# A two-model transformer forward on one core: the last MLP's second product with tokens on the output partitions

## The reference

```python
h = h + jnp.square(jax.nn.relu(rmsnorm(h, g) @ w_up)) @ w_down   # w_up [1024, 4096], w_down [4096, 1024]
return h * rsqrt(mean(h * h, axis=-1) + 1e-6) * final_norm_g
```

## Time and profile before

| | us |
|---|---|
| median of 3 runs | 1107.19 (1106.84 to 1107.58) |
| profiled execution | 1107.31 |
| its span | 1105.6 |
| TensorE busy | 1095.7 (99%) |
| VectorE busy | 780.3 (71%) |
| ScalarE busy | 608.8 (55%) |
| w1's first product, last product's start | 1006.55, 1095.59 |

### The profile page before, as it was taken

The page is one execution under the profiler, slowest core; times in us unless marked ns, Lnnn a source line. Parts: engine busy times, 40 slices in busy tenths (PEclk is TensorE's granted clock), DMA queues, the critical chain, the costliest instruction groups (busy, mean ns, idle before and its releaser), DMA issues.

```text
span 1105.6 us, 19232 instructions
## 1 busy us (share of the span) xinstructions
PE 1095.7 (99%) x7572; PEld 1001.8 (91%) x7572; DVE 780.3 (71%) x981; ACT 608.8 (55%) x825; POOL 214.9 (19%) x222
## 2 busy tenths in 40 slices
PE   9999999999999999999999999999999999999997
PEld 9999988889888888999999888888899998888886
DVE  7657985886877755799985777754477667776443
ACT  6667557645555543775763556643344446665332
POOL 2996003302000000177843110000010001000001
PEclk9999999999999999999999999999999999999999
DMA  9774442655555555445500455555545445655541
GB/s 296 223 234 153 154 149 96 231 172 191 191 190 190 190 192 189 150 157 191 191 2 1 152 159 190 188 211 189 185 162 178 156 139 166 210 191 190 190 152 39
DMA packets 155058, 187.30 MB, mean 169 GB/s; under 512 B 6608, under 2 KB 143984, under 8 KB 154992
## 3 DMA queue, kind: packets, MB, share of 16 engines
q1 hardware_dynamic: 151152, 183.80, 50.4%
q10 hardware_dynamic: 3840, 2.57, 0.8%
HBM read 185.29 MB, written 1.07 MB: 169 GB/s over the span
## 4 chain that ended last, share of the span: by engine, by line
PE 95%; DVE 2%; ACT 1%; DMA 0%; issue 0%; POOLq 0%; ACTq 0%; DVEq 0%
PE PS L478 24%; PE PS L528 12%; PE PS L483 12%; PE PS L407 9%; PE PS L408 8%; PE PS L409 8%; PE PS L530 6%; PE PS L355 2%; PE PS L488 1%; PE PS L490 1%; PE PS L489 1%; PE PS L880 1%; PE PS L2206 1%; PE PS L2219 1%; PE PS L858 1%; DVE WL L403 1%
## 5 line engine op out<-in xcount | busy, mean ns | idle before, releaser
L403 DVE TENSOR_TENSOR WL<-RAW,WH 128x2048 fp32r<-128x2048 f32 x169 | 394.7, 2337 | 190.3 <-ACT WH L394 189.7
L394 ACT ACTIVATE WH<-RAW 128x2048 fp32r<-128x2048 f32 x169 | 322.9, 1911 | 186.5 <-PE PS L530 121.1
L478 PE MATMUL PS<-XHL,WH 128*128 128x512 f32 x976 | 336.4, 395 | 0.2 <-DVE WL L403 0.2
L483 PE MATMUL PS<-XHL,WL 128*128 128x256 f32 x976 | 262.2, 278 | 0.0
L478 PEld LDWEIGHTS PS<-XHL,WH 128*128 128x128 f32 x976 | 179.3, 188 | 38.1 <-DVE WL L403 0.4
L528 PE MATMUL PS<-HHL,WH 128*128 (+1 forms) x592 | 205.4, 394 | 0.0
L407 PE MATMUL PS<-XHL,WH 128*128 128x256 f32 x656 | 188.9, 288 | 0.0
L483 PEld LDWEIGHTS PS<-XHL,WL 128*128 128x128 f32 x976 | 183.6, 188 | 4.9
L408 PE MATMUL PS<-XHL,WH 128*128 128x256 f32 x656 | 185.9, 283 | 0.0
L409 PE MATMUL PS<-XHL,WL 128*128 128x256 f32 x656 | 185.9, 283 | 0.0
L530 PE MATMUL PS<-HHL,WL 128*128 (+1 forms) x592 | 164.4, 278 | 0.0
(11 more groups left out here) (344 smaller groups left out, 1668.9 us busy)
## 6 DMA issues: line engine op xcount, KB each, us to landing
RAW<-in_mlp_w_up SPq DMA_DIRECT2D x32, 1024.0 KB, 5.4
RAW<-in_mlp_w_down SPq DMA_DIRECT2D x32, 1024.0 KB, 4.9
RAW<-in_w_in SPq DMA_DIRECT2D x24, 1024.0 KB, 5.1
RAW<-in_w_ffn_in_pairs SPq DMA_DIRECT2D x22, 1024.0 KB, 5.1
RAW<-in_dn_w_in SPq DMA_DIRECT2D x16, 1024.0 KB, 6.0
RAW<-in_mb_w_in SPq DMA_DIRECT2D x12, 1024.0 KB, 5.1
RAW<-in_w_ffn_out SPq DMA_DIRECT2D x11, 1024.0 KB, 4.8
RAW<-in_w_in SPq DMA_DIRECT2D x16, 256.0 KB, 6.1
```

Of the source, the lines that this page charges most:

```text
L394: act.activation(WH[:, k], RAW[:, k], ACT.Copy).then_inc(hi_done, 1)
L403: dve.tensor_tensor(WL[:, k], RAW[:, k], WH[:, k].bitcast(F32), ALU.subtract).then_inc(lo_done, 1)
L478: pe.matmul(out, h[:, k, part], both[:, k].rearrange("p e t -> p (e t)"), start=(k == 0), stop=False, skip_group_check=True)
L483: mm = pe.matmul(out[:, TOK:512], l[:, low, part], both[:, low, 0], start=False, stop=(low == KB - 1), skip_group_check=True)
```

## The change

Only w1 and what follows it change. Hidden activations are the stationary operand now and the split weights move, so w1's sums have 128 tokens on the partitions and features along the row: token block t takes banks 2t and 2t+1. The residual `H` must be turned to be added: VectorE turns it in 32 x 32 blocks, 32 instructions of [32 partitions, 8 x 32], three behind each split, into `HT` [128, 2, 1024]. The last two chunks are ordered by token block; the second token block's last 512 features are two pieces of 256 in banks 6 and 7, beside bank 3, which holds their earlier chunks. Squares are summed along the rows by ScalarE's accumulator, one column for each piece; a root and a reciprocal for each token block give a per-partition factor. The norm's weight is loaded as a row on all partitions (`GROW`, 512 KB, behind the weights on SyncE's queue). The output is stored as [256, 1024], in four pieces. TensorE's sums and turned rows, and all of GpSimd's part of the end, go.

```diff
+        def token_terms(pe, st, k, t, c0, n, start=False, stop=False, bank_=None):
+            at = st.j * KROWS + k
+            xh, xl = HHL[:, at, 0, t * P:t * P + P], HHL[:, at, 1, t * P:t * P + P]
+            wide = [(PS[:, 2 * t + c // 512 if bank_ is None else bank_, 0:min(n, 512)],
+                     slice(k * D + c, k * D + c + min(n, 512))) for c in range(c0, c0 + n, 512)]
+            for out, w in wide:
+                pe.matmul(out, xh, WH[:, st.slot, w], start=start, stop=False, skip_group_check=True)
+            for out, w in wide:
+                pe.matmul(out, xh, WL[:, st.slot, w], start=False, stop=False, skip_group_check=True)
+            for out, w in wide:
+                mm = pe.matmul(out, xl, WH[:, st.slot, w], start=False, stop=stop, skip_group_check=True)
+            return mm
+        def multiply_tokens(pe, st, ready, wide):
+            pe.wait_ge(lo_done, st.count())
+            pe.wait_ge(s_.hl_done, ready)
+            first = st.j == 0
+            for k in range(KROWS):
+                for t in range(TT):
+                    if first and k == 0 and t == 1:
+                        wide_bank_read(pe, wide, 2)
+                    mm = token_terms(pe, st, k, t, 0, D, start=first and k == 0)
+            mm.then_inc(mm_done, 1)
+        def multiply_tokens_end(pe, last, ready):
+            ends = (Step(last.seg, last.j - 1, None), last)
+            for t in range(TT):
+                for st in ends:
...
+                    if st is not last:
+                        for k in range(KROWS):
+                            mm = token_terms(pe, st, k, t, 0, D)
+                        if t:
+                            mm.then_inc(s_.rows_done, 1)
+                        continue
+                    for t_, c0, n, bank_ in OUT_PIECES:
+                        if t_ == t:
+                            for k in range(KROWS):
+                                mm = token_terms(pe, st, k, t, c0, n, start=bank_ > 3 and k == 0, stop=k == KROWS - 1, bank_=bank_)
+                            mm.then_inc(s_.out_rows, 1)
-        OUT_PIECES = ((0, 1), (1, 1), (2, 2), (4, 2))
+        OUT_PIECES = ((0, 0, 512, 0), (0, 512, 512, 1), (1, 0, 512, 2), (1, 512, 256, 6), (1, 768, 256, 7))
+        def piece_squares(act, i):
+            act.wait_ge(s_.out_added, i + 1)
+            act.activation(spare, HT[:, t, c0:c0 + n], ACT.Square, scale=1.0 / 32,
+                           accum_out=SQS[:, i:i + 1]).then_inc(s_.sq_done, 1)
@@ sync: behind the last weight chunk
+            sp.wait_ge(mm_done, seg["u1"].first + seg["u1"].n)
+            sp.dma_start(GROW[:], a["final_g"].partition_broadcast(P)).then_inc(s_.row_in, 16)
+            for i, (t, c0, n, _) in enumerate(OUT_PIECES[:3]):
+                sp.wait_ge(s_.out_scaled, i + 1)
+                sp.dma_start(a["out"][t * P:t * P + P, c0:c0 + n], OUT[:, t, c0:c0 + n]).then_inc(s_.out_done, 16)
@@ scalar: the end
+            piece_squares(act, 0)
+            piece_squares(act, 1)
+            act.wait_ge(s_.out_part, 1)
+            act.activation(SDC[:, 0:1], SQ2[:, 0:1], ACT.Sqrt, bias=EPSC[:], scale=1.0).then_inc(s_.sd_done, 1)
+            piece_squares(act, 2)
+            piece_squares(act, 3)
+            piece_squares(act, 4)
+            act.wait_ge(s_.out_part, 2)
+            act.wait_ge(s_.sq_done, 4 * NORMS + 5)
+            act.activation(SDC[:, 1:2], SQS[:, 4:5], ACT.Sqrt, bias=SQ2[:, 1:2], scale=1.0).then_inc(s_.sd_done, 1)
+            act.wait_ge(s_.out_weighed, 2)
+            act.wait_ge(s_.rc_ready, NORMS + 2)
+            act.activation(OUT[:, 1, 512:D], OUT[:, 1, 512:D], ACT.Copy, scale=RC[:, 1:2]).then_inc(s_.out_last, 1)
+            act.wait_ge(s_.out_last, 1)
+            act.dma_start(a["out"][P:TOK, 512:D], OUT[:, 1, 512:D]).then_inc(s_.out_done, 16)
@@ vector: w1
+                for st in (Step(w, j, None) for j in range(w.n)):
+                    if st.j < w.n - 2:
+                        split_lo(dve, st)
...
+                    for t, q, i in turns_[3 * st.j:3 * st.j + 3]:
+                        to = HT[32 * q:32 * q + 32, t].rearrange("p (b c) -> p b c", b=KB)[:, :, 32 * i:32 * i + 32]
+                        ch(dve.transpose(to, H[32 * i:32 * i + 32, :, t * P + 32 * q:t * P + 32 * q + 32]))
@@ vector: the end (piece_added: HT += PSUM; piece_weighed: OUT = HT * GROW; piece_scaled: OUT = HT * RC * GROW)
+            piece_added(0)
+            piece_added(1)
+            dve.wait_ge(s_.sq_done, 4 * NORMS + 2)
+            dve.tensor_tensor(SQ2[:, 0:1], SQS[:, 0:1], SQS[:, 1:2], ALU.add).then_inc(s_.out_part, 1)
+            token_inverse(0)
+            piece_scaled(0)
+            piece_scaled(1)
+            dve.wait_ge(s_.rows_done, 3 * len(row_no) + 1)
+            ch(dve.tensor_tensor(HT[:, 1, 512:D], HT[:, 1, 512:D], PS[:, 3], ALU.add))
+            piece_added(2)
+            ch.wait(dve)
+            piece_added(3)
+            piece_weighed(3)
+            piece_added(4)
+            dve.wait_ge(s_.sq_done, 4 * NORMS + 4)
+            dve.scalar_tensor_tensor(out=SQ2[:, 1:2], in0=SQS[:, 2:3], scalar=EPS, in1=SQS[:, 3:4],
+                                     op0=ALU.add, op1=ALU.add).then_inc(s_.out_part, 1)
+            piece_weighed(4)
+            token_inverse(1)
+            piece_scaled(2)
```

More of the change, by code:

```diff
@@ new lines, in multiply_tokens @@
+        def multiply_tokens(pe, st, ready, wide):
[12 more added lines that the diff above has]
+                for st in ends:
+                    if t == 0:
+                        pe.wait_ge(lo_done, st.count())
+                        pe.wait_ge(s_.hl_done, ready - (st is not last))
+                    if st is not last:
[9 more added lines that the diff above has]
+                            mm.then_inc(s_.out_rows, 1)
@@ L625, in norm_sums @@
         def norm_sums(pe, m):
[L628 to L637, removed]
+            if m == 2:
                 pe.wait_ge(s_.prep, 1)
@@ L755, in add_rows @@
             dve.wait_ge(s_.low_added, 4 * row_no[sg.name])
-            for b in range(4 if m != FINAL else 3):
+            for b in range(4):
                 if b < 3:
@@ L1353, in row_chunks @@
                 split_hi(act, Step(w, w.n - 1, None))
-                if m == FINAL:
-                    return final_pieces(act)
-                for p in range(4):
+                for p in range(4 if m < NORMS else 0):
                     norm_high(act, m, p)
@@ L2042, in _, with piece_added @@
             mlp(1)
[L2043 to L2050 removed]
+            def piece_added(i):
+                t, c0, n, bank_ = OUT_PIECES[i]
+                dve.wait_ge(s_.out_rows, i + 1)
+                dve.tensor_tensor(HT[:, t, c0:c0 + n], HT[:, t, c0:c0 + n], PS[:, bank_, 0:n], ALU.add).then_inc(s_.out_added, 1)
@@ new lines, in token_inverse @@
+            def token_inverse(t):
+                dve.wait_ge(s_.sd_done, NORMS + 2 + t)
+                dve.reciprocal(RC[:, t:t + 1], SDC[:, t:t + 1]).then_inc(s_.rc_ready, 1)
+            ch.wait(dve)
+            dve.wait_ge(s_.row_in, 64)
+            piece_added(0)
[4 more added lines that the diff above has]
+            piece_scaled(0)
@@ L2320, in mlp @@
             def mlp(layer):
-                steps(pe, seg[f"u{layer}"], times_x_wide(3 + 2 * layer), head=3)
+                u = seg[f"u{layer}"]
+                steps(pe, u, times_x_wide(3 + 2 * layer), head=3)
                 w = seg[f"w{layer}"]
-                steps(pe, w, lambda st: multiply_rows(pe, st, st.local(HBASE[f"u{layer}"]), seg[f"u{layer}"]), head=1, tail=SLOTS)
+                if layer == 0:
+                    return steps(pe, w, lambda st: multiply_rows(pe, st, st.local(HBASE["u0"]), seg["u0"]), head=1, tail=SLOTS)
+                for st in (Step(w, j, None) for j in range(w.n - 2)):
+                    multiply_tokens(pe, st, st.local(HBASE["u1"]), u)
+                last = Step(w, w.n - 1, None)
+                multiply_tokens_end(pe, last, last.local(HBASE["u1"]))
             mlp(0)
@@ L2346, in _ @@
             mlp(1)
-            norm_sums(pe, FINAL)
-            pe.wait_ge(s_.rc_ready, FINAL + 1)
-            for b, signal in ((2, s_.rows_ready), (3, s_.rows_again)):
-                for c in range(TT):
-                    mm = pe.transpose(PS[:, b, c * P:(c + 1) * P], RC[:, c:c + 1].to_broadcast([P, P]), IDENT[:])
-                mm.then_inc(signal, 1)
 _VECTORS = [name for name, _ in VECTORS]
```

113 lines of the change are left out of this document (39 added, 74 removed).

## The result

| | before | changed |
|---|---|---|
| median, same chip | 1107.33 (6 runs) | 1101.16 (6 runs, 1100.84 to 1102.53) |
| profiled execution, span | 1107.31, 1105.6 | 1101.25, 1099.5 |
| w1, first to last product's start | 89.04 | 87.02 |
| last product's start to last store's issue | 5.77 | 2.86 |
| ScalarE's store (the last of the program) from its issue to the span's end | 4.2 | 3.0 |

The ratio is 0.9946, 95% interval 0.9935 to 0.9956. Of the 6.1 us of span, 2.0 come from TensorE's stream, 2.9 from the work behind it, and 1.2 from the stores; the start of w1 is 0.04 us later.

What follows compares the result with a forecast made beforehand. TensorE, busy 1095.7 of 1105.6 us, was taken to bound the kernel. Stream 0.0 and tail -3.1 us, against the median of 1107.19, gave 1104.1 us; the range was 1101.9 to 1106.0.

Steps and rivals of the forecast that it cites:

- The price of a 512-column product: TensorE's stream in w1: 0.232 us each, bounds 0.2283 and 0.2333, so the stream gains nothing.
- K: Theory of the experiments, from rival A: a product costs its columns at 2.4 GHz plus 13.3 ns, in any role.
- rival A: w1's stream: products cost columns at 2.4 GHz plus 13.3 ns; 2.0 us more go, 1102.1; chance 0.17.
- The last store's issue: Tail: both last stores issued at about L' + 2.75, against L + 5.49 before; 2.74 us less.
- L': Modelled end of w1's last product in the changed kernel; L is the same end before the change.
- Rival B: Tail: VectorE's queue holds it, token block 0's scaled pieces standing in front; gain 1.6 us, 1105.6; chance 0.13.
- The stores: Tail: the last two stores land in 3.4 us, between 3.0 and 3.8, and the span ends 0.43 later.
- the tail's upper bound of 3.6: Behind w1's last product: the most the tail could gain in us, against 3.15 forecast and 2.0 as lower bound.
- the turns' cost: VectorE in w1: 32 block turns of 32 x 256 elements at 0.42 us each.
- their cover: VectorE in w1: a turn of up to 1.32 us stays hidden and delays nothing; cost zero.
- SyncE's load of the norm's weights: SP's 512 KB load goes out some 28 us before VectorE wants it; cost zero.
- Rival C: w1's stream: 512-column products cost more when 24 stand in a row; at 0.250 us each 1110.9; chance 0.08.

Runs made afterwards that it cites:

- e1: Changed kernel plus ten rows of 24 extra products, of various widths and roles, in w1's chunk 5, into unread banks: 1144.38 us.
- e3: Changed kernel with every 512-column product of w1's chunks 1 to 14 cut into two of 256 columns: 1105.56 us.
- e9: Changed kernel without the two scaled products of token block 0, which is stored unscaled: 1100.86 us.
- e12: Changed kernel with VectorE adding piece 4 before it weighs piece 3: 1100.98 us.
- e5: Changed kernel with the stores of the first two pieces held until the last reciprocal is there: 1101.94 us.
- e10: Changed kernel with five stores, all once the last reciprocal is there, in count, size and 1 KB rows as before the change: 1102.88 us.
- e7: Changed kernel with each block turn done twice, 64 turns in all: 1101.14 us.
- e8: Changed kernel with each block turn done four times, twelve behind each split: 1125.81 us.
- e6: Changed kernel with each 256 KB store cut into two with rows of 1 KB, at the same moments: 1101.30 us.

## Why the prediction was wrong

**The price of a 512-column product** is the step that failed in the stream: 0.232 us was taken, 0.2267 measured. It was read as half the distance from the start of two 512s to that of the 256s behind them, and called measured directly. But what was known was the group's total, 0.6967. At K's prices the two 512s are 0.4533 of it and the two 256s 0.2400, and 3.4 ns are left over. The distance, 0.4664, is 13 ns above that 0.4533: the 3.4 ns, and some 10 ns that the distances take off the 256s (0.2303 instead of 0.2400), as in e1's pairs. The lower bound of 0.2283 put the 3.4 ns on the 512s too, so both bounds lay above the true price. The constant form (rival A) had been worked out from pairs and from runs of 256s with the same 13.3 ns twice, which was the better evidence: it takes only totals of repeated patterns. It got a chance of 0.17. A said 87.1 us for w1; 87.02 + 0.12 were measured. This step is worth 2.0 us, and e1 to e3 show it.

The page cited beside it (the Trainium skill, TensorE: Matmul & The Clock Gate, "Back-to-back issue gap") gives that form for an isolated product, with a constant of 2.5 ns. In these fp32r streams the form holds from 256 columns up, with 13.3 ns (0.2267 us for 512 columns, 0.1200 for 256). The section's figure for a stream, about 131 ns for 512 columns, shows in no run here.

**The last store's issue** was put at L' + 2.75 and came at +2.58. The prices were right: 0.75 for a scaled piece against 0.76 taken, 0.63 and 0.40 to 0.42 for squares, 0.19 for the sum, 0.29 for the root against 0.26. The order was right too. The 0.17 us are mostly VectorE's queue: its last add was to start 0.4 us after the last product's end and started 0.19 after it. The forecast had put that delay down to token block 0's scaled products as well; e9 shows that they cost nothing, and e12 that the weighing of piece 3 makes the 0.15 us that remain beyond a handing over. Rival B had the wrong culprit, and its prices did not come either (0.75 for a scaled piece instead of 0.9, some 0.04 for a handing over instead of 0.1).

**The stores** were the other mis-sized term, and the step that failed in the tail: landing 3.4 taken, 3.0 as the lower bound, 2.7 measured. With what lies behind the landing it is 3.0 instead of 3.83 from the last issue to the end. The bound came from a store that itself had others in front of it, with rows of 1 KB. In the changed kernel SyncE's first two stores of 256 KB, alone in the queue, landed in 2.1 us, and the two last ones, beside each other, in 2.4 and 2.7. e5 and e10 show that stores in front and shorter rows with one more store bring the 1.2 us back; how it was shared out before the change stays open.

The stream gave 2.0 us more than forecast and the tail 1.0 (4.1 against 3.15). The stream alone would have come to A's 1102.1, inside the range; only with the tail did the time pass it. The range did not cover its own terms here: A together with the tail's upper bound of 3.6 is 1101.6. That the time was lower still came from the stores, whose lower bound was too high.

**What held:** the turns' cost (0.42 taken, 0.436 measured) and their cover, to twice their number (e7), with the price beyond it of the right kind and 7% too low (e8); SyncE's load of the norm's weights at nothing (issued at 1065.9, landed in 5.7 us, first used at 1090.6); straight-line code of TensorE at nothing; no gap between 1006 and 1094. Rival C is refuted by e1: 24 products of 512 columns in a row cost 0.2267 in either role. Two smaller things in the turns' account were off. The cover was reckoned with VectorE's first split 1.9 us into w1, where it starts at 5.3 (e8), so a turn could have cost some 1.2 us and not 1.32. And the estimate of 10 us from the Trainium skill (VectorE: DVE Perf Modes, "The three transpose paths") took the figure for a block of 128 columns once for each turn, though a turn has 256. The 32 turns took 13.9 us.

## What to carry to other kernels

Price a product from the total of a repeated pattern of one length, never from the distance between starts inside a mixed one; with two lengths and a constant, two such totals settle it. At equal columns count the products: here each one less saved 13.3 ns, so fewer and longer ones are worth looking for where TensorE sets the time. Take the landing of a last store from one that had the queue to itself, and ask what the change takes out from in front of it.

## What the runs showed of the hardware that was not expected

- fp32r products: 0.2267 us for 512 columns, 0.1733 for 384, 0.1200 for 256, but 0.113 for 192 and 0.110 for 128, where the columns alone would be 0.080 and 0.053; a 128-column product beside a 512 still costs its 0.11.
- The same stationary operand or another (loaded for each product in both), the weights moving or standing, one bank or two: no difference at 512 columns (0.2263 to 0.2271).
- Two or more 512s followed by a 256 cost 3 to 17 ns a group over the sum of the prices.
- With all DMA engines busy, stores in rows of 2 KB moved 379 and 385 GB/s and in rows of 1 KB 343 and 346, with a short queue (the changed kernel, e6) as with a long one (e5, e10). With the short queue it showed in the time by 0.2 us at most.
- A 32 x 256 block turn on VectorE takes 0.436 us.
